# A streaming encoder step on eight cores: the head of the kernel is put in another order

## What is computed

```python
h = rmsnorm(x, g_pre)
xa, ba, ca, za, xb, zb, ga, gb = split(h @ w_in)      # eight sections of 1024 columns
u = ca * xa
conv = conv_b + sum(conv_w[k] * up[:, k:k + L] for k in range(3))
ya = ((ba * conv) * silu(za)) @ w_a_out
d = trailing_mean(xb, W_g) - xb                       # windows 2, 4, 8, 16 by channel group
yb = ((d @ w_grp[g]) * pool_scale * silu(zb)) @ w_b_out
m = sigmoid(ga) * ya + sigmoid(gb) * yb
x1 = x + rmsnorm(m @ w_o, g_post)
out = x1 + (p @ w_ple) * sigmoid(x1 @ w_pgate)
```

## Time and profile before

| | |
|---|---|
| median of 3 runs | 782.38 us |
| profiled execution | 782.25 us |
| its span, slowest core (core 5) | 780.7 us |
| spans of the 8 cores | 778.1 to 780.7 us |
| TensorE busy | 751.0 us, 96% |
| VectorE, ScalarE, GpSimd busy | 43%, 34%, 41% |
| first transposes on TensorE | 9.90 us |
| first section matmul | 25.56 us |

### The profile page before, as it was taken

One profiled execution on the slowest core, in us unless ns is written; L12 is line 12 of the kernel. 1 busy time (PEld: TensorE's weight loads), 2 busy tenths in 40 slices (PEclk: granted clock), 3 DMA queues, 4 the chain that ended last, 5 costly groups with the idle time before them and its releaser, 6 DMA issues.

```text
span 780.7 us, 13187 instructions; the slowest of 8 cores (778.1 to 780.7 us)
## 1 busy us (share of the span) xinstructions
PE 751.0 (96%) x4101; PEld 366.4 (47%) x4101; DVE 336.1 (43%) x527; ACT 262.9 (34%) x461; POOL 321.9 (41%) x466
## 2 busy tenths in 40 slices
PE   1799999999999999999999999999999999999996
PEld 0344444444444444444454555545555555554443
DVE  2454445443522211599644555455451212115534
ACT  3532222323333321465433233332322121225553
POOL 3333444556543433264432244555563332213452
PEclk9999999999999999999999999999999999999999
DMA  8799667657898659456254347542565553001432
GB/s 202 181 149 143 82 101 111 90 78 108 166 179 182 114 80 231 93 195 210 82 82 54 45 66 112 80 54 39 74 114 101 79 77 55 1 1 67 150 108 108
DMA packets 36835, 82.89 MB, mean 106 GB/s; under 512 B 4121, under 2 KB 5410, under 8 KB 36770
## 3 DMA queue, kind: packets, MB, share of 16 engines
q0 software_dynamic: 26960, 48.31, 42.8%
q1 hardware_dynamic: 9810, 33.76, 13.6%
HBM read 121.09 MB, written 9.27 MB: 167 GB/s over the span
## 4 chain that ended last, share of the span: by engine, by line
PE 95%; DMA 2%; DVE 1%; issue 1%; ACT 0%; SPq 0%; POOL 0%; DVEq 0%; ACTq 0%; POOLq 0%
PE ps L574 44%; PE ps L733 30%; PE ps L789 8%; PE ps L845 7%; DMA arena<-xp 2%; PE ps L692 2%; PE ps L856 2%; PE ps L550 2%; PE ps L829 1%; DVE hb L868 0%; SPq L394 0%; PE ps L890 0%; PE ps L421 0%; DVE hb L901 0%; DVE hT L490 0%
## 5 line engine op out<-in xcount | busy, mean ns | idle before, releaser
L574 PE MATMUL ps<-hT,ring 128*128 128x512 bf16 (+1 forms) x1872 | 345.5, 346 | 0.0
L574 PEld LDWEIGHTS ps<-hT,ring 128*128 128x128 bf16 x1872 | 166.9, 98 | 174.6
L733 PE MATMUL ps<-hT,ring 128*128 128x512 bf16 (+1 forms) x640 | 124.2, 347 | 0.0
L297 POOL DMA_DIRECT2D ring<-w_in x128 | 69.6, 546 | 88.3 <-PE ps L574 66.9
L755 DVE TENSOR_TENSOR arena<-ps,arena 128x512 f32<-128x512 f32 (+1 forms) x40 | 24.4, 611 | 149.6 <-PE ps L733 100.7
L763 POOL TENSOR_TENSOR mT<-arena 128x512 bf16<-128x512 f32 (+1 forms) x40 | 44.3, 1108 | 103.5 <-DVE arena L759 103.0
L733 PEld LDWEIGHTS ps<-hT,ring 128*128 128x128 bf16 x640 | 57.6, 98 | 60.3
L649 POOL TENSOR_TENSOR arena<-XB 128x526 f32<-128x526 f32 (+1 forms) x40 | 40.0, 1001 | 108.2 <-ACT XB L628 94.3
L872 POOL TENSOR_TENSOR arena<-hb,arena 128x512 f32<-128x512 f32 x30 | 50.8, 1694 | 40.7 <-DVE hb L868 39.4
L745 ACT ACTIVATE arena<-ps 128x512 f32<-128x512 f32 (+1 forms) x40 | 21.3, 533 | 134.3 <-PE ps L733 134.3
L733 PE MATMUL ps<-qT,ring 128*128 128x512 bf16 (+1 forms) x320 | 65.4, 347 | 0.0
(11 more groups left out here) (92 smaller groups left out, 698.5 us busy)
## 6 DMA issues: line engine op xcount, KB each, us to landing
ring<-w_in POOLq DMA_DIRECT2D x128, 256.0 KB, 5.9
arena<-xp SPq DMA_DIRECT2D x32, 512.0 KB, 6.7
yp<-arena SPq DMA_DIRECT2D x16, 512.0 KB, 2.9
ring<-w_a_out POOLq DMA_DIRECT2D x16, 256.0 KB, 6.1
ring<-w_b_out POOLq DMA_DIRECT2D x16, 256.0 KB, 6.2
wo_sb<-w_o POOLq DMA_DIRECT2D x8, 256.0 KB, 5.9
wpg_sb<-w_pgate POOLq DMA_DIRECT2D x8, 256.0 KB, 5.3
U<-xT SPq DMA_DIRECT2D x3, 512.0 KB, 5.9
```

The source lines that it names most:

```text
L297: OP('pool', lambda e, d: d(e.dma_start(out=ring[:, slot, :, :], in_=ring_seq[i])), writes=[ring_res[slot]], dma=f"ring{slot}")
L574: ins = e.matmul(bank(bi)[:, 0:N], lhsT=sl[:, kk, :], rhs=hT[:, kk, k.rel:k.rel + N], start=(kk == 0), stop=(kk == 7))
L733: ins = e.matmul(bank(bi)[:, 0:N], lhsT=sl[:, kk, :], rhs=act[:, kk, k.rel:k.rel + N], start=(kk == 0), stop=(kk == 7))
```

## The change

The head is no longer sorted by nominal times; its order is written out.

- Three waits are built in: the first section load waits for x tile 1 to have landed, and x tiles 4, 5, 6 and 7 wait for sections 0, 2, 3 and 4 to have landed (tile 7 takes the place of tile 4).
- g_pre is loaded as one row of 4 KB into gpost_bc and spread to 128 partitions by two float32 matmuls with a row of ones, each copied to row_bc by VectorE. gpost, and smallT with the cached rows, are loaded after j = 3 of phase 1. The channel vectors, g_pre among them, get a tensor of their own, vecT (24 KB), which is loaded behind x tile 3.
- The matmuls of the first two units are cut into pieces by rows (`phase1_pieces`): the first block's XA and CA into rows 0 to 383 and 384 to 511, the second block's into pieces of 128 and 256 rows, put between the transposes of tiles 4 to 7. Both units use banks 0 to 5; transposes use banks 6 and 7.
- Groups of 20, 8, 12 and 10 matmuls of 128 columns, whose result is not used, stand between the transposes of tiles 0 to 3 (`keep_warm`).
- `phase1_unit` takes a table `between`, and calls its functions at named places of the first unit's element-wise work. The norms of tiles 4 and 5 and their copies stand there, those of tiles 6 and 7 behind the unit.
- Copies to hT are all on VectorE but for that of tile 2. The stats tile is zeroed earlier. Mean and root have become helper functions, without a change in what they issue.

```diff
+        def load_gpre():
+            OP('sp', lambda e, d: d(e.dma_start(out=gpost_bc[0:1, :], in_=g_pre[0:1, :])), writes=[res("gpost")], dma="ld_gpost")
+
+        def spread_gpre():
+            for h in range(2):
+                b = balloc(1, [6, 7])
+                OP('pe', lambda e, d, b=b, h=h: d(e.matmul(bank(b), lhsT=ones_f[0:1, :], rhs=gpost_bc[0:1, h * 512:(h + 1) * 512], start=True, stop=True)),
+                   reads=[res("ones_f"), res("gpost")], writes=[pres[b]])
+                OP('dve', lambda e, d, b=b, h=h: d(e.tensor_copy(out=row_bc[:, h * 512:(h + 1) * 512], in_=bank(b))), reads=[pres[b]], writes=[res("row_bc")])
+
+        def keep_warm(n):
+            def f(e, d):
+                ins = None
+                for _ in range(n):
+                    ins = e.matmul(bank(5)[:, 0:128], lhsT=ident_b[:], rhs=ident_b[:], start=True, stop=True)
+                d(ins)
+            OP('pe', f, reads=[res("ident_b")], writes=[pres[5]])
...
-        def load_section():
+        def load_section(after=()):
...
-            OP('pool', lambda e, d: d(e.dma_start(out=ring[:, slot, :, :], in_=ring_seq[i])), writes=[ring_res[slot]], dma=f"ring{slot}")
+            OP('pool', lambda e, d: d(e.dma_start(out=ring[:, slot, :, :], in_=ring_seq[i])), reads=list(after), writes=[ring_res[slot]], dma=f"ring{slot}")
...
-                s.w = alloc('xt_head', [0, 1, 2, 3, 4, 5])
+                s.w = (0, 1, 2, 3, 4, 5, 6, 4)[gi]
...
-                OP('sp', lambda e, d: d(e.dma_start(out=wap(s.w), in_=tl.x)), writes=wres(s.w), dma=f"ldW{s.w}")
+                OP('sp', lambda e, d: d(e.dma_start(out=wap(s.w), in_=tl.x)), reads=list(after), writes=wres(s.w) + [res(f"land{gi}")], dma=f"ldW{s.w}")
...
-                if gi % 2 == 0:
+                if gi == 2:
...
-            return [(base, a), (base + 2.3, b), (base + 3.6, c), (base + 4.0, c2), (base + 4.8, dd), (base + 6.4, ee), (base + 7.2, ff)]
+            return a, b, c, dd, ee, ff
...
+        def phase1_pieces(k):
+            banks = {}
+
+            def piece(sec, c0, c1):
...
+                def f(e, d):
+                    ins = None
+                    for kk in range(8):
+                        ins = e.matmul(bank(bi)[:, c0 - k.rel:c1 - k.rel], lhsT=sl[:, kk, :], rhs=hT[:, kk, c0:c1], start=(kk == 0), stop=(kk == 7))
+                    d(ins)
...
+        k0, k1 = sb_info[0].blocks
+        after = {4: ring_res[0], 5: ring_res[2], 6: ring_res[3], 7: ring_res[4]}
+        tiles = [phase0_ops(tl, [after[tl.gi]] if tl.gi in after else []) for tl in sb_info[0].tiles]
+        ld, sq, rt, dd, tr, hc = ([t[q] for t in tiles] for q in range(6))
+        p0, p1 = phase1_pieces(k0), phase1_pieces(k1)
...
+        seq(load_gpre, ld[0], ld[1], ld[2], ld[3], setup_vec, spread_gpre,
+            sq[0], rt[0], lambda: load_section([res("land1")]), load_section, dd[0], warm(20), tr[0],
+            sq[1], rt[1], load_section, dd[1], hc[0], warm(8), tr[1],
+            sq[2], rt[2], dd[2], hc[1], warm(12), tr[2],
+            sq[3], rt[3], load_section, load_section, hc[2], dd[3], warm(10),
+            part(p0, 0, 384, S_XA), tr[3], hc[3], part(p0, 0, 384, S_CA), part(p0, 384, 512, S_XA, S_CA), part(p0, 0, 512, S_BA),
+            ld[4], ld[5])()
+        phase1_unit(0, sb_info[0], 0, k0, pre_banks=list(range(6)), between={
+            'xa': seq(sq[4], rt[4], load_section),
+            'u': seq(dd[4], part(p0, 0, 512, S_ZA), tr[4], ld[6], ld[7]),
+            'conv': seq(hc[4], part(p1, 512, 640, S_XA, S_CA), part(p0, 0, 512, S_XB)),
+            'xb': seq(sq[5], part(p0, 0, 512, S_ZB)),
+            'win': seq(rt[5], load_section, load_section, dd[5], tr[5], hc[5], part(p1, 640, 768, S_XA, S_CA),
+                       part(p1, 512, 768, S_BA, S_ZA, S_XB))})
+        seq(sq[6], rt[6], load_section, load_section, dd[6], tr[6], hc[6], part(p1, 512, 768, S_ZB), part(p1, 768, 896, S_XA),
+            sq[7], rt[7], load_section, load_section, dd[7], tr[7], hc[7], part(p1, 768, 896, *secs[1:]), part(p1, 896, 1024, *secs))()
```

More of the change, by code:

```diff
@@ L151, in build_program @@
         ident_b = sb("ident_b", [128, 128], BF16)
-        smallT = sb("smallT", [128, 8, 74], F32)
+        ones_f = sb("ones_f", [128, 128], F32)
+        vecT = sb("vecT", [128, 8, 6], F32)
+        smallT = sb("smallT", [128, 8, 68], F32)
         row_bc = sb("row_bc", [128, 1152], F32)
@@ L402, in c @@
             def c():
[L403 to L408, removed]
+                mean_sq(0, gi)
+                inv_root(0, gi)
             def dd():
@@ L535, in build_program, with phase1_unit, then @@
         pending_b2 = []
[L537 to L550, removed]
-                                           start=(kk == 0), stop=(kk == 7))
-                        d(ins)
-                    OP('pe', f, reads=[slr] + hres(k, 0), writes=[pres[bi]])
-                items.append((t0 + dt * g, fn))
-            return items, banks
-        def phase1_unit(sbi, info, j, k, pre_banks=None):
+        def phase1_pieces(k):
+            banks = {}
+            def piece(sec, c0, c1):
+                if sec not in banks:
+                    banks[sec] = (S_XA, S_CA, S_BA, S_ZA, S_XB, S_ZB).index(sec)
+                    claim(pres[banks[sec]], 1)
+                bi = banks[sec]
+                sl, slr = section(0, 1, 0, sec)
+                def f(e, d):
[3 more added lines that the diff above has]
+                    d(ins)
+                rr = [res(f"hT_t{t}_{kk}") for t in range(c0 // 128, c1 // 128) for kk in range(8)]
+                assert all(r.epoch == 0 for r in rr)
+                OP('pe', f, reads=[slr] + rr, writes=[pres[bi]])
+            return piece
+        def phase1_unit(sbi, info, j, k, pre_banks=None, between=None):
+            between = between or {}
+            def then(name):
+                if name in between:
+                    between[name]()
             N = k.N
@@ L584, in phase1_unit @@
             b_xa, b_ca, b_ba, b_za, b_xb, b_zb = banks
-            cw = lambda t: smallT[:, j, t:t + 1]
-            cbias = smallT[:, j, 3:4]
-            psc = smallT[:, j, 4:5]
-            sm = res("smallT")
+            cw = lambda t: vecT[:, j, t:t + 1]
+            cbias = vecT[:, j, 3:4]
+            sm = res("vecT")
             ur = ures("U", k)
@@ L607, in phase1_unit @@
                reads=[pres[b_xa]], writes=[tres[t_xa]])
+            then('xa')
             OP('dve', lambda e, d: d(e.tensor_tensor(out=uwin(U, k, 16, E), in0=blkview(bank(b_ca), k),
@@ L610, in phase1_unit @@
                reads=[pres[b_ca], tres[t_xa]], writes=[ur])
+            then('u')
             t_c = alloc('c', [2, 3])
@@ L620, in phase1_unit @@
                reads=[ur, sm, tres[t_c]] + prev_u, writes=[tres[t_c]])
+            then('conv')
             t_sz = alloc('sz', [4, 5])
@@ L655, in phase1_unit @@
                 tsel ^= 1
+            then('win')
             if last:
@@ L704, in flush_q @@
                 OP('dve', lambda e, d, bb=bb, jj=jj, k=k: d(e.scalar_tensor_tensor(
-                    out=actview(qT, jj, k), in0=blkview(bank(bb), k), scalar=smallT[:, jj, 4:5],
+                    out=actview(qT, jj, k), in0=blkview(bank(bb), k), scalar=vecT[:, jj, 4:5],
                     in1=actview(mT, jj, k), op0=ALU.mult, op1=ALU.mult)),
-                   reads=[pres[bb], res("smallT"), ares("mT", jj, k)], writes=[ares("qT", jj, k)])
+                   reads=[pres[bb], res("vecT"), ares("mT", jj, k)], writes=[ares("qT", jj, k)])
         def flush_b2():
@@ L987, in build_program @@
         nsb = len(SBS)
-        items = []
-        for n, tl in enumerate(sb_info[0].tiles):
-            items += phase0_ops(tl, n * P0_PERIOD)
         def load_sections(n):
@@ new lines, in build_program, with seq, run, part @@
+        tiles = [phase0_ops(tl, [after[tl.gi]] if tl.gi in after else []) for tl in sb_info[0].tiles]
+        ld, sq, rt, dd, tr, hc = ([t[q] for t in tiles] for q in range(6))
+        p0, p1 = phase1_pieces(k0), phase1_pieces(k1)
+        def seq(*fns):
+            def run():
+                for fn in fns:
+                    fn()
+            return run
+        def part(p, c0, c1, *secs):
+            return lambda: [p(sec, c0, c1) for sec in secs]
+        warm = lambda n: (lambda: keep_warm(n))
@@ L1006, in build_program @@
                 for k in info.order:
-                    phase1_unit(sbi, info, j, k, pre_banks=pre_banks0 if (sbi, j, k.idx) == (0, 0, 0) else None)
+                    if (sbi, j, k.idx) != (0, 0, 0):
+                        phase1_unit(sbi, info, j, k, pre_banks=list(range(6)) if (sbi, j, k.idx) == (0, 0, 1) else None)
                     if resident_loads and (j, k.idx) != (0, 0):
```

90 lines of the change are left out of this document (46 added, 44 removed).

## The result

The changed kernel takes 787.67 us, the median of 5 runs (787.14 to 788.9), against 782.66 for the kernel before beside it: a ratio of 1.0063, 95% interval 1.0047 to 1.0078. It is 5.0 us slower; the forecast was 780.0 with a range of 776.5 to 784.0.

What follows compares the result with a forecast made beforehand. TensorE, busy 96% of the span, was taken as the bound, so only its head waits and slow stretches could be won: E = 15.5 + 32.4 = 47.9, 2.35 us earlier, 782.25 - 2.35 = 779.9 (780.0 against the median), range 776.5 to 784.0.

Steps and rivals of the forecast that it cites:

- E: Start of unit j=1 on TensorE, 50.25 us in the kernel before; forecast 47.9, 2.35 earlier, everything after it unchanged.
- T: Start of the first section matmul on TensorE, 25.56 us in the kernel before; forecast 15.5.
- (c): Rival at section 0's load: again 11.4 us from issue, T 18.9, E 51.3, time 783.4, 785.5 with (b); chance 0.15.
- x tile 4 lands T+5.2: First block's loads: x tile 4, issued when section 0 lands, is in 5.2 us after T.
- (b): Rival at TensorE's waits around tile 5's transposes: clock falls, matmuls cost 2.1 us more, time 782.1; chance 0.20.
- Transposes 5 T+19.4, TensorE waits 3.5 and 0.95 us: Second block: tile 5's norm queues behind ScalarE's copy of XB and Silu of ZB; TensorE waits 3.5 and 0.95 us.
- x tiles 1 to 3 landing by 10 us: Sign of being right, head loads: with g_pre at 4 KB, tiles 1 to 3 land at 6.3, 7.7 and 9.1.

Runs made afterwards that it cites:

- e2_warm_fill: Changed kernel with 142 more unused matmuls in the waits before and behind the transposes of tiles 4 and 5; 783.71 us, ratio 1.0015.
- e3_norm5_early: Changed kernel with tile 5's square and mean emitted behind the convolution, its transposes and copy behind ZB; 782.00 us, ratio 0.9993.
- three mendings: Changed kernel with x tiles 4, 5 tied to tile 3's landing, 6, 7 to sections 0, 2; tile 5's norm earlier; unused matmuls in remaining waits; 779.29 us.
- ties staggered: Changed kernel with the three mendings, but x tile 5 tied to section 0, 6 to section 2, 7 to section 3; 777.93 us, ratio 0.9940.
- e1_untied: Changed kernel with x tiles 4 to 7 no longer waiting for weight sections to land; 787.59 us, ratio 1.0063.
- e11_row_warm_no_copy: Kernel before with g_pre as one row and unused matmuls, tile 3's copy left behind tile 4's scale; 779.38 us, ratio 0.9954.

## Why the prediction was wrong

Point by point, E of core 4 against E of the forecast, 55.5 and 47.9, 7.6 us:

- **T.** 15.5 forecast, 16.2 measured, 0.7 us. That section 0 landed at 15.1, where 15.3 was forecast, is luck: it was issued at 8.64 and not at 7.3, and took 6.5 us and not 8.0. It was the copy of tile 2 that ended last, its x tile having come later than forecast. The feared rival (c), section 0 as late as in the kernel before, did not come, since no x tiles were queued ahead of it.
- **x tile 4.** "x tile 4 lands T+5.2" was wrong: it landed at T+7.7, and its transposes ended at T+12.1 and not T+9.8. With the copy behind them 2.4 us. I had let a tile issued at section 0's landing share the engines at once; on core 4 four sections stood in the other queue, and in the microsecond from 18 on the x queue moved one packet. On core 5 the tile took 5.6 us, near the 5.4 of the forecast; on the other six 6.2 to 8.1.
- **The clock.** "The clock falls" stood as rival (b), with a chance of 0.20 and a price of 2.1. It came twice and cost 3.7 us, and e2_warm_fill, with the clock held, gave 4.0 us back. This is the largest error. The forecast itself held waits of 1.7 and 3.5 us, and the earlier trace rows has slow matmuls behind a wait of 3.56; I had no row for the opposite and still gave it the likelier side.
- **The order.** "Transposes 5 T+19.4, TensorE waits 3.5 and 0.95 us" was right as a mechanism and in size (3.61 and 1.05, ended by VectorE behind GpSimd's root behind ScalarE). Taking it away (e3_norm5_early) gave 5.7 us, since the second fall of the clock went with it.
- **The loads.** "x tiles 1 to 3 landing by 10 us" was too early: they landed at 8.1, 10.2 and 11.8, where I had 6.3, 7.7 and 9.1 by the best rate of the earlier trace rows. That is still 2.6 us sooner for tile 1 than in the earlier trace rows, and the row alone in the old order gave 3.3 us. The change contained its gain, and lost it together with 5 us more.
- The remaining 0.8 us are spread over the hand-overs of the second half and were not followed singly.

Apart from (c), which was also priced with (b), the rivals were priced one at a time. The waits that one creates were the cause of the other, so (b) belonged into the forecast, and with it and tile 4's landing the sum would have been 48.6 + 2.4 + 3.7 = 54.7. The Trainium skill (TensorE: Matmul & The Clock Gate, Why this matters for your kernels) warns of idle gaps between bursts of matmuls; the granted clock of 0.50 behind the waits of 4.07 and 1.57 us agrees.

## What to carry to other kernels

An earlier start of the bottleneck engine, here by 9.4 us, is worth nothing by itself; follow the chain of every later piece of data in the order of each engine, because a norm written behind a unit's copy waits for that unit, whatever has landed. Before an order is rebuilt, try its cheapest part in the old order: one row instead of a broadcast gave 3.3 us, more than the rebuilt head gave in any but its mended forms. The old order with the row, the copy moved and unused matmuls (0.9945) came as far as the rebuilt one with its three mendings and the ties staggered (0.9940). Price a wait on TensorE together with the slower matmuls behind it, and fill it with work, at the place where it stands.

## What the runs showed of the hardware

- A transfer that enters behind a loaded queue of another engine may not share at once. x tile 4 of the changed kernel, issued with sections outstanding, moved its first packet 1.0 to 3.6 us after its issue and took 5.6 to 8.6 us over the eight cores; x tiles 0 and 7 of core 4, issued with no and with one section outstanding, took 4.4. With x tiles ahead, section 0 took 9.3 to 10.5 us on the eight cores of e1_untied and 11.4 in the kernel before; with none, 4.4 to 6.5. Once both queues are running they share about evenly: from 18 to 24 us in the kernel before, 41 to 53% of the engines' time for the sections and 42 to 56% for x. The Trainium skill (DMA: Bandwidth & Descriptors, Queues, rings and completion order) describes engines that take turns between queues packet by packet; the traces agree for the steady state, and on cores 0 and 4 not for the first 3.6 us of the newcomer. Why is not shown.
- The two float32 matmuls of 512 columns with one row of weights are recorded as four and take 3.75 us in all; two copies included, row_bc stood at 7.2 us, where the forecast had 7.5.
- The granted clock column stayed at 1.00 in the head before, though its first matmuls ran at 420 ns; in e11_row_warm_no_copy it shows 0.54 for the same stretch with the same busy time of 3.57 us, and in the changed kernel 0.50 for one of the same kind. The spacing of the matmuls is the surer reading.
